# Masks and sink columns of a sliding-window attention section moved from VectorE to half-row TensorE products

## The chip, the cores and the metric

One Trainium2 chip, of which the kernel uses one core. The metric is the device time of one execution in microseconds; lower is better. A core has TensorE (PE, with the loading of its stationary operand shown apart as PEld), VectorE (DVE), ScalarE (ACT), GpSimd (POOL) and SyncE (SP), which run in parallel and meet at semaphores.

## What is computed

Two transformer blocks, one after the other, on 512 tokens of width 1024 in float32. The first has a gated linear attention, a pooling branch and a mixture of 16 experts. The second block has two layers, and each layer runs three attention branches, a cross attention to a memory of 256 tokens, and a gated feed-forward part. The change touches only the first branch of each of these two layers, a sliding-window attention of 8 heads with a window of 128 and one learned sink per head:

```python
mask = (kpos <= t) & (kpos > t - window) & (kpos >= 0)
s = jnp.einsum('bqgrd,bkgd->bgrqk', qb, kb).astype(jnp.float32) * (d ** -0.5)
p = masked_probs(s, mask, sink)      # the sink joins the maximum and the denominator
o = jnp.einsum('bgrqk,bkgd->bqgrd', p.astype(vb.dtype), vb)
```

With blocks of 128 queries, a block sees its own 128 keys under a causal mask and the 128 keys before it under the opposite mask ("recent": only those keys count whose place in their block is after the query's place in its own). The first block has no block before it.

## The kernel before

The kernel is one program with an instruction stream written out by hand for each engine. Attention is cut into units. `units()` (L525) lists them for one layer: section 0 is the sliding-window branch and has 16 units, in the order query block 3, 2, 1, 0 and within a block the head pairs t = 0 to 3. A unit computes two heads, `side` 0 and 1, whose scores lie in two PSUM banks. Twelve units have 256 keys (`nk` 256), the last four have 128. Section 1 (28 units of the sparse branch), section 2 (latent attention) and section 3 (cross attention) follow later in the layer.

Each of PE, DVE and ACT has its own `attend(sec)` that walks over the units in steps s. A step of PE (L1324) issues, in this order:

- the score products of unit s: for each side one product of 64 rows (side 0 on rows 0 to 63, side 1 on rows 64 to 127) and nk columns, then `scored`;
- the transposes of unit s-2, two for each block of keys and side (L1352), after a wait for `scaled` of that unit;
- the products of the probabilities with the values for unit s-3, after a wait for `turned_out`;
- in steps 0, 1, 3, 4, 8 and 9 of section 0, half of a tile of the value projection (`v_behind`, four products of 408 columns, operands `ring,h`).

After step 16 of section 0 come four products of the next stage (`merge_head`), then the last two units, then `merge`. A float32 product appears in the trace as two loads and two matmuls, a transpose as one of each.

A step of DVE (L2533) for unit s in section 0 adds the mask to both sides in PSUM (L2559), copies the two sink values into column nk of the two banks (L2573), drains, and takes the negated row maximum over nk + 1 columns (L2578, `biased`). Then for unit s-1 it waits for `exped`, takes the reciprocal of the sum (L2599) and scales the probabilities (L2605, `scaled`). In steps 1, 5 and 10 it also copies a finished value tile. ACT takes the exponential of unit s (L1763) and copies the transposed probabilities of unit s-1 out of PSUM (L1773).

Section 1 already leaves its causal mask to PE: `barred` is true there, and four more products on 64 rows each add it to the scores in PSUM. Two of them have 128 columns and two have 64; the stationary operand is the upper or lower half of the identity (`ident`) or of the identity turned by 64 (`crossed`), and the moving operand is a half of the rows of the mask itself (`cst`). The products of side 0 use rows 0 to 63 and those of side 1 rows 64 to 127.

Of the kernel before, what the change touches and what calls it, by code (L numbers as in the profile page):

```python
# [17 lines left out]
ALU = mybir.AluOpType  # L18
# [3 lines left out]
P = 128  # L22
# [14 lines left out]
MASKED = -1e30  # L37
# [122 lines left out]
def columns(parts):  # L160
    at, n = {}, 0
    for name, width in parts:
        at[name] = (n, width)
        n += width
    return at, n


CST, N_CST = columns([("ident", P), ("ones", P), ("recent", P), ("causal", P), ("barred", 64), ("crossed", P),
                      ("cmp_add", TT * CB), ("freq", 1), ("freqM", 1),
                      ("sign", 1), ("signM", 1), ("eps", 1), ("eps2", 1)])  # L170
CS1, N_CS1 = columns([("maskf", P), ("maskb", P), ("scan", 768)])
# [8 lines left out]
def constants():  # L180
    c = np.zeros((P, N_CST), np.float32)
    r = np.arange(P)

    def put(arr, at, name, v):
        o, w = at[name]
        arr[:, o:o + w] = v

    put(c, CST, "ident", np.eye(P))
    put(c, CST, "ones", 1.0)
    put(c, CST, "barred", MASKED)  # L190
    put(c, CST, "crossed", np.roll(np.eye(P), 64, axis=0))
    put(c, CST, "causal", np.where(r[None, :] <= r[:, None], 0.0, MASKED))
    put(c, CST, "recent", np.where(r[None, :] > r[:, None], 0.0, MASKED))
    t = np.arange(T).reshape(TT, P)
    ok = (16 * np.arange(NCMP)[None, None, :] + 31) <= t[:, :, None]
    add = np.full((TT, P, CB), MASKED / 10, np.float32)
    add[:, :, 0:NCMP] = np.where(ok, 0.0, MASKED)
    put(c, CST, "cmp_add", add.transpose(1, 0, 2).reshape(P, -1))
    f = (np.float32(10000.0) ** (-np.arange(32, dtype=np.float32) / np.float32(32))).astype(np.float32)
    put(c, CST, "freq", f[r % 32][:, None])  # L200
    f = (np.float32(10000.0) ** (-np.arange(16, dtype=np.float32) / np.float32(16))).astype(np.float32)
    put(c, CST, "freqM", f[r % 16][:, None])
    put(c, CST, "sign", np.where(r % 64 < 32, -1.0, 1.0)[:, None])
    put(c, CST, "signM", np.where(r % 32 < 16, -1.0, 1.0)[:, None])
    put(c, CST, "eps", EPS)
    put(c, CST, "eps2", EPS * EPS)
    c1 = np.zeros((P, N_CS1), np.float32)
    same = (r[:, None] // CHUNK) == (r[None, :] // CHUNK)
    put(c1, CS1, "maskf", same & (r[:, None] <= r[None, :]))
    put(c1, CS1, "maskb", same & (r[:, None] >= r[None, :]))  # L210
    put(c1, CS1, "scan", (np.arange(768) % CHUNK != 0)[None, :])
    ce = np.zeros((P, N_CSE), np.float32)
    put(ce, CSE, "iota", np.arange(CAP)[None, :])
    put(ce, CSE, "cidx", (r % CAP)[:, None])
    sel = np.zeros((P, 8, P), np.float32)
    for p in range(8):
        sel[2 * p, p, :64] = 1.0
        sel[2 * p + 1, p, 64:] = 1.0
    put(ce, CSE, "pairsel", sel.reshape(P, -1))
    inv = np.zeros((4, ROWS, COLS), np.float32)  # L220
    for i, w in enumerate(WINDOWS):
        n = [np.clip(np.arange(m) + w // 2, 0, m) - np.clip(np.arange(m) - w // 2, 0, m) for m in (ROWS, COLS)]
        inv[i] = 1.0 / (n[0][:, None] * n[1][None, :])
    return c, c1, ce, np.ascontiguousarray(np.broadcast_to(inv.reshape(1, -1), (P, 4 * T)))


def two_blocks(nc, stream, xT_d, ctxT_d, memT_d, pos_d, cst_d, cs1_d, cse_d, inv_d, pr1_d, pr2_d, out_d):
    ctx = ExitStack()
    with ctx:
# [10 lines left out]
        cst = sb("cst", [P, N_CST])  # L240
# [169 lines left out]
        def c_(name):  # L410
            o, w = CST[name]
            return cst[:, o:o + w]
# [112 lines left out]
        def units():  # L525
# [5 lines left out]
            def pair(sec, qt, nk, kind, qk, values, outs, first=True, final=True, sink=None, gate=None, end=False, joins=False):  # L531
                nb = nk // P
                u, j = (out[-1], 1) if joins else (None, 0)
                pv = [(outs[i][0], outs[i][1], values[i][b], i, slice(nk * j + P * b, nk * j + P * b + P),
                       first and b == 0, final and b == nb - 1)
                      for b, i in ([(b, i) for b in range(nb) for i in range(2)] if sec < 3 else
                                   [(b, i) for i in range(2) for b in range(nb)])]
                barred = sec == 1
                s = [[(i, slice(nk * j, nk * j + nk), q, k, part is qk[0] and j == 0, part is qk[-1] and not barred)
                      for i, (q, k) in enumerate(part)] for part in qk]  # L540
                if barred:
                    low, high, o, to = slice(0, 64), slice(64, P), CST["causal"][0], nk * (j + 1)
                    s.append([(0, slice(to - P, to), c_("ident")[low, :], cst[low, o:o + P], False, False),
                              (1, slice(to - P, to), c_("crossed")[high, :], cst[high, o + 64:o + 64 + P], False, False),
                              (0, slice(to - 64, to), c_("crossed")[low, :], cst[low, o:o + 64], False, True),
                              (1, slice(to - 64, to), c_("ident")[high, :], cst[high, o + 64:o + P], False, True)])
                if joins:
                    u["subs"], u["nb"], u["end"] = 2, 2 * nb, end
                    u["s"] = [a + b for a, b in zip(u["s"], s)]
                    u["gate"] = u["gate"] and u["gate"] + [gate]  # L550
                    u["pv"] += pv
                    return
                out.append(dict(sec=sec, qt=qt, nk=nk, nb=nb, subs=1, kind=kind, sink=sink, gate=gate and [gate], end=end,
                                s=s, pv=pv))
# [1373 lines left out]
        def _(dve):  # L1928
# [575 lines left out]
            for l in range(LAYERS):  # L2504
# [22 lines left out]
                def attend(sec, between=None):  # L2527
# [7 lines left out]
                    for s in range(len(us) + 1):  # L2535
                        if s < len(us):
# [17 lines left out]
                                                  ALU.add).then_inc(biased, 1)  # L2554
                            else:
                                w = nk
                                if u["kind"] == "window":
                                    o = CST["causal"][0] + P - nk
                                    dve.tensor_tensor(S[:, :, 0:nk], S[:, :, 0:nk],  # L2559
                                                      cst[:, o:o + nk].rearrange("p (g c) -> p g c", g=1)  # L2560
                                                      .to_broadcast([P, 2, nk]), ALU.add)
                                elif u["kind"] == "causal" and u["sec"] == 2:
                                    if u["subs"] == 1:
                                        dve.tensor_tensor(S[:, :, nk - P:nk], S[:, :, nk - P:nk],
                                                          c_("causal").rearrange("p (g c) -> p g c", g=1)
# [4 lines left out]
                                                          .to_broadcast([P, 2, 2, P]), ALU.add)  # L2570
                                if u["sink"] is not None:
                                    w = nk + 1
                                    dve.tensor_copy(S[:, :, nk:w], p2("sinks").rearrange("p (g t) -> p g t", g=2)  # L2573
                                                    [:, :, u["sink"]:u["sink"] + 1])
                                if u["sec"] in (0, 2):
                                    dr()  # L2576
                                if u["subs"] == 1:
                                    ins = dve.tensor_reduce(nbias[:, n % 4, 0:2], S[:, :, 0:w], AX.X, ALU.max, negate=True)  # L2578
# [580 lines left out]
```

## Time and profile before

| | us |
|---|---|
| median of 3 runs | 3275.41 |
| the three runs | 3275.16, 3275.41, 3279.26 |
| the profiled execution, its own time | 3284.84 |
| span of its trace, first to last instruction | 3283.0 |
| PE busy in that span | 3187.8 (97%) |
| DVE busy | 1488.1 (45%) |
| section 0 of the first layer in the trace | from 1078.6 to about 1134.8 |
| section 0 of the second layer in the trace | from 2195.6 to about 2254.0 |

Times in the rows below are microseconds from the span's start in the one profiled execution. The profiled execution took 9.43 us longer than the median of the runs. In a row of the timeline the second number is how long the merged group lasted, from the start of its first to the end of its last instruction, so neighbouring groups overlap; the distance between two starts is what the argument uses. The granted clock of 1.00 is 2.4 GHz, 0.50 is 1.2 GHz.

### The profile page before, as it was taken

The page shows a single profiled execution, that of the slowest core. Times are in us where ns is not written, and L with a number is a line of the kernel's source. Part 1 is how long each engine was busy: PE and PEld are TensorE (multiplying, and loading weights), DVE is VectorE, ACT ScalarE, POOL GpSimd, SP SyncE. Part 2 cuts the span into 40 slices and gives each one's busy share as a digit, 9 for nine tenths or more (in the row PEclk, how much of TensorE's full clock was granted, in tenths as well). Part 3 has the DMA queues.
Part 4 walks back from the last instruction along what each step waited for, and adds up shares of the span by engine and source line. Part 5 has one row for each costly group of instructions (what it writes and reads, how often), then busy time and mean ns, then how long its engine had stood idle before and what let it go on. Part 6 is the DMA issues. An engine that isn't in the chain of part 4 may idle for free.

```text
span 3283.0 us, 39520 instructions
## 1 busy us (share of the span) xinstructions
PE 3187.8 (97%) x15880; PEld 2133.4 (65%) x15880; DVE 1488.1 (45%) x2914; ACT 677.7 (21%) x1393; POOL 142.6 (4%) x100
## 2 busy tenths in 40 slices
PE   7999999999999899999999999999999999999998
PEld 2445784444433575855865888857578478578887
DVE  2244663221113645736634454446375376255533
ACT  2032221000003415423021000023271231210000
POOL 3400010000000000000000000000000000000000
PEclk9999999999999899999999999999999999999999
DMA  7241247999995121121221222311201112222221
GB/s 298 100 160 40 77 170 302 409 406 387 404 409 225 45 84 52 40 77 33 77 90 68 87 89 87 106 62 65 96 9 69 66 52 83 72 77 87 94 84 71
DMA packets 120149, 435.86 MB, mean 133 GB/s; under 512 B 13216, under 2 KB 15008, under 8 KB 119200
## 3 DMA queue, kind: packets, MB, share of 16 engines
q1 hardware_dynamic: 114768, 417.91, 34.1%
q10 hardware_dynamic: 5200, 15.43, 1.2%
q8 instruction: 127, 2.08, 0.3%
q14 instruction: 54, 0.44, 0.0%
HBM read 429.09 MB, written 4.19 MB: 132 GB/s over the span
## 4 chain that ended last, share of the span: by engine, by line
PE 92%; DVE 4%; ACT 2%; issue 1%; DVEq 1%; DMA 1%; ACTq 0%; SPq 0%
PE bank L688 90%; PE bank L1352 1%; DMA ring<-in_stream 1%; DVE arena L2578 1%; DVE arena L2605 0%; DVE arena L2580 0%; DVE bank L2559 0%; DVE arena L2142 0%; PE bank L1347 0%; ACT arena L1722 0%; DVEq L2576 0%; ACT arena L1798 0%; DVE arena L2179 0%; PE bank L1195 0%; DVE arena L2608 0%
## 5 line engine op out<-in xcount | busy, mean ns | idle before, releaser
L688 PE MATMUL bank<-arena 128*128 128x256 f32 (+12 forms) x5520 | 931.3, 375 | 32.7 <-issue 9.7
L688 PEld LDWEIGHTS bank<-arena 128*128 128x128 f32 (+4 forms) x5520 | 624.2, 172 | 290.3 <-issue 166.8
L688 PE MATMUL bank<-h,ring 128*128 128x256 f32 (+1 forms) x1936 | 630.8, 477 | 1.6 <-issue 1.3
L688 PEld LDWEIGHTS bank<-h,ring 128*128 128x128 f32 x1936 | 365.6, 191 | 224.5 <-issue 192.7
L688 PE MATMUL bank<-arena,ring 128*128 128x256 f32 (+2 forms) x1872 | 498.3, 419 | 3.3 <-DVE y L2064 1.8
L688 PEld LDWEIGHTS bank<-arena,ring 128*128 128x128 f32 (+1 forms) x1872 | 332.9, 186 | 151.0 <-issue 107.4
L688 PE MATMUL bank<-ring,arena 128*64 128x512 f32 (+2 forms) x976 | 227.4, 603 | 18.0 <-ACT arena L1568 11.7
L688 PE MATMUL bank<-y,arena 128*128 128x256 f32 (+1 forms) x1064 | 239.0, 381 | 0.0
L688 PE MATMUL bank<-y,ring 128*128 128x256 f32 (+1 forms) x800 | 227.1, 439 | 0.0
L688 PEld LDWEIGHTS bank<-y,arena 128*128 128x128 f32 x1064 | 202.1, 190 | 29.2 <-issue 1.9
L1923 POOL TENSOR_TENSOR sq<-sq 128x512 f32<-128x512 f32 (+1 forms) x56 | 75.1, 1342 | 3072.1 <-ACT sq L1549 3072.1
L688 PEld LDWEIGHTS bank<-y,ring 128*128 128x128 f32 x800 | 151.9, 190 | 69.0 <-issue 53.8
L688 PEld LDWEIGHTS bank<-ring,arena 128*64 128x64 f32 (+2 forms) x976 | 70.8, 137 | 159.5 <-issue 138.0
L1763 ACT ACTIVATE arena<-bank,arena 128x256 f32<-128x256 f32 (+5 forms) x288 | 141.9, 506 | 127.1 <-DVE arena L2578 77.0
L1549 ACT ACTIVATE sq<-x 128x512 f32<-128x512 f32 x64 | 40.1, 630 | 423.1 <-DVEq L2882 256.8
L1773 ACT ACTIVATE arena<-bank 128x1024 f32<-128x1024 f32 (+3 forms) x120 | 92.7, 772 | 118.0 <-PE bank L1352 112.9
L2481 DVE TENSOR_TENSOR arena<-arena,bank 128x512 f32<-128x512 f32 x16 | 11.0, 689 | 194.2 <-PE bank L688 194.2
L688 PE MATMUL bank<-h,arena 128*128 128x256 f32 (+2 forms) x408 | 94.5, 475 | 0.8 <-ACT arena L1722 0.8
L1935 DVE COPY arena<-bank 128x512 f32<-128x512 f32 (+4 forms) x51 | 33.4, 654 | 135.3 <-PE bank L688 132.9
L2892 DVE TENSOR_TENSOR x<-x,bank 128x256 f32<-128x256 f32 x48 | 20.2, 421 | 160.0 <-PE bank L688 159.4
L2578 DVE TENSOR_REDUCE arena<-bank 128x2 f32<-128x514 f32 (+3 forms) x80 | 72.4, 905 | 33.3 <-PE bank L688 29.7
L1352 PE MATMUL bank<-cst,arena 64*128 64x64 f32 x1216 | 61.5, 233 | 19.5 <-DVE arena L2605 16.2
(327 smaller groups left out, 2770.6 us busy)
## 6 DMA issues: line engine op xcount, KB each, us to landing
ring<-in_stream SPq DMA_DIRECT2D x581, 512.0 KB, 4.5
arena<-in_stream SPq DMA_DIRECT2D x132, 512.0 KB, 13.1
h<-in_stream SPq DMA_DIRECT2D x42, 512.0 KB, 11.9
sig<-in_stream SPq DMA_DIRECT2D x21, 512.0 KB, 11.9
sq<-in_stream SPq DMA_DIRECT2D x21, 512.0 KB, 12.3
x<-in_xT ACTq DMA_DIRECT2D x1, 2048.0 KB, 11.2
arena<-memory_kv ACTq DMA_DIRECT2D x4, 512.0 KB, 6.8
outT<-h ACTq DMA_DIRECT2D x8, 256.0 KB, 2.1
```

Of the source, the lines that this page charges most:

```text
L688: ins = pe.matmul(out, lhsT, rhs, start=start, stop=stop, skip_group_check=loose)
L1352: ins = pe.transpose(bank[:, 4 + i, at:at + 64], probs[r, n % 3, side, P * b:P * b + P], c_("ident")[r, r])
L1549: act.activation(sq[:, min(k, 1), 0:width], src(k), ACT.Square).then_inc(squared, 1)
L1763: ins = act.activation(probs[:, n % 3, side, c], bank[:, 2 * (n % 2) + side, c], ACT.Exp, bias=nbias[:, n % 4, i:i + 1], accum_out=den[:, ...
L1773: act.activation(probsT[:, n % 2, :, 0:P * u["nb"]], bank[:, 4:6, 0:P * u["nb"]], ACT.Copy).then_inc(turned_out, 1)
L1923: pool.tensor_tensor(sq[:, 0, 0:width], sq[:, 0, 0:width], sq[:, 1, 0:width], ALU.add).then_inc(added, 1)
L1935: dve.tensor_copy(out, N.bank(n)[0:m, 0:width] if src is None else src).then_inc(N.taken_sem, 1)
L2481: dve.tensor_tensor(acts[:, 512 * half:512 * half + 512], sg[:, half, :], bank[:, 2 + half, :], ALU.mult).then_inc(a_ready, 1)
L2578: ins = dve.tensor_reduce(nbias[:, n % 4, 0:2], S[:, :, 0:w], AX.X, ALU.max, negate=True)
L2892: dve.tensor_tensor(xq[:, part, :], xq[:, part, :], bank[:, b, 0:H2], ALU.add).then_inc(down_taken, 1)
```

## The change

The constants get one more field, `barred_low`: 64 columns of the mask value, ahead of `recent`, so that the shifted slices of `recent` can be read as the ones of `causal` are. `barred` becomes true for section 0 too. For a unit with 256 keys four products add the recent mask on the first 128 key columns (128, 64, 64 and 128 columns); for every unit with a sink four products of one column write the two sinks into column nk; then the four causal products follow, as in section 1. DVE no longer adds the window mask, no longer copies the sinks, and no longer drains in section 0. Its reduction over nk + 1 columns and everything else stay.

```diff
-CST, N_CST = columns([("ident", P), ("ones", P), ("recent", P), ("causal", P), ...
+CST, N_CST = columns([("ident", P), ("ones", P), ("barred_low", 64), ("recent", P), ("causal", P), ...
+    put(c, CST, "barred_low", MASKED)
...
-                barred = sec == 1
+                barred = sec < 2
...
                 if barred:
                     low, high, o, to = slice(0, 64), slice(64, P), CST["causal"][0], nk * (j + 1)
+                    same, other = [c_("ident")[r, :] for r in (low, high)], [c_("crossed")[r, :] for r in (low, high)]
+                    if kind == "window" and nk == 2 * P:
+                        s.append([(0, slice(0, P), other[0], cst[low, o - P - 64:o - 64], False, False),
+                                  (1, slice(0, 64), other[1], cst[high, o - 64:o], False, False),
+                                  (0, slice(0, 64), same[0], cst[low, o - P:o - 64], False, False),
+                                  (1, slice(0, P), same[1], cst[high, o - P:o], False, False)])
+                    if sink is not None:
+                        s.append([(i, slice(nk, nk + 1), block_, p2("sinks")[r, 4 * i + sink:4 * i + sink + 1], False, False)
+                                  for blocks_ in ((same[0], other[1]), (other[0], same[1]))
+                                  for i, (r, block_) in enumerate(zip((low, high), blocks_))])
...
-                                if u["kind"] == "window":
-                                    o = CST["causal"][0] + P - nk
-                                    dve.tensor_tensor(S[:, :, 0:nk], S[:, :, 0:nk],
-                                                      cst[:, o:o + nk].rearrange("p (g c) -> p g c", g=1)
-                                                      .to_broadcast([P, 2, nk]), ALU.add)
-                                elif u["kind"] == "causal" and u["sec"] == 2:
+                                if u["kind"] == "causal" and u["sec"] == 2:
...
                                 if u["sink"] is not None:
                                     w = nk + 1
-                                    dve.tensor_copy(S[:, :, nk:w], p2("sinks").rearrange("p (g t) -> p g t", g=2)
-                                                    [:, :, u["sink"]:u["sink"] + 1])
-                                if u["sec"] in (0, 2):
+                                if u["sec"] == 2:
                                     dr()
```

## Rows read from the trace of the kernel before

**Rows 1.** The page: what the chain that ended last is made of.

```profile
PE 92%; DVE 4%; ACT 2%; issue 1%; DVEq 1%; DMA 1%; ACTq 0%; SPq 0%
```

**Rows 2.** Timeline, a step with value products beside it and the next without (PE loads).

```profile
1097.23 0.30 PEld L688 LDWEIGHTS bank<-arena 64*128 64x128 f32 x4 [0.58 <-issue]
...
1098.10 0.42 PEld L688 LDWEIGHTS bank<-arena 128*64 128x64 f32 x8 
...
1098.69 0.30 PEld L688 LDWEIGHTS bank<-arena 64*128 64x128 f32 x4 [0.17 <-issue]
```

**Rows 3.** Timeline of a later step of section 0, first layer.

```profile
1100.64 0.69 DVE L2559 TENSOR_TENSOR bank<-bank,cst 128x512 f32<-128x512 f32 x1 
...
1101.46 0.69 DVE L2578 TENSOR_REDUCE arena<-bank 128x2 f32<-128x514 f32 x1 
...
1102.27 0.62 DVE L2605 TENSOR_SCALAR arena<-arena 128x256 f32<-128x256 f32 x2 
...
1102.80 0.69 DVE L2559 TENSOR_TENSOR bank<-bank,cst 128x512 f32<-128x512 f32 x1 
...
1102.94 0.33 PEld L1352 LDWEIGHTS bank<-cst,arena 64*128 64x128 f32 x8 [1.37 <-DVE arena L2605]
```

**Rows 4.** Waits in section 0, first layer: us in total, times, longest.

```profile
PEld bank L1352 <- DVE arena L2605: 9.5, 8, 2.0
```

**Rows 5.** The same of section 0 of the second layer.

```profile
PEld bank L1352 <- DVE arena L2605: 9.0, 8, 2.0
```

**Rows 6.** DVE's groups by form in 1078 to 1133: busy us, mean ns; idle before.

```profile
L2559 DVE TENSOR_TENSOR bank<-bank,cst 128x512 f32<-128x512 f32 x12 | 8.3, 693 | 9.4 <-PE bank L688 9.4
...
L2573 DVE COPY bank<-arena 128x2 f32<-128x2 f32 x16 | 2.4, 152 | 0.0
...
L2559 DVE TENSOR_TENSOR bank<-bank,cst 128x256 f32<-128x256 f32 x4 | 1.7, 430 | 2.0 <-PE bank L688 2.0
```

**Rows 7.** Timeline of PE loads in section 1, a joined unit with eight mask products.

```profile
1345.46 0.98 PEld L688 LDWEIGHTS bank<-cst 64*128 64x128 f32 x16 
1346.30 0.38 PEld L1352 LDWEIGHTS bank<-cst,arena 64*128 64x128 f32 x8 
```

**Rows 8.** Timeline of PE loads: eight score products of 32 columns on 64 rows.

```profile
1293.35 0.97 PEld L688 LDWEIGHTS bank<-arena 64*128 64x128 f32 x16 [0.17 <-issue]
1294.34 0.57 PEld L1352 LDWEIGHTS bank<-cst,arena 64*128 64x128 f32 x16 
1294.97 0.14 PEld L688 LDWEIGHTS bank<-arena 128*64 128x64 f32 x2 
```

**Rows 9.** Timeline: four products of 16 columns on 128 rows, in the first block.

```profile
485.24 1.04 PE L688 MATMUL bank<-arena,tmp 128*128 128x16 f32 x8 [0.91 <-DVE tmp L2383]
```

**Rows 10.** Windows: length, busy us (instructions) of PE, PEld, DVE, ACT, POOL, granted clock, DMA share, GB/s.

```profile
1117.00:1119.70 2.70, 1.66 (x20) 1.23 (x20) 2.52 (x9) 2.09 (x6) 0.00 (x0) 0.79 0.95 357
1119.70:1132.20 12.50, 11.65 (x76) 8.26 (x72) 6.04 (x25) 5.93 (x22) 0.00 (x0) 0.50 0.16 65
...
1134.80:1141.00 6.20, 6.17 (x21) 5.16 (x22) 5.33 (x10) 1.19 (x3) 0.00 (x0) 0.72 0.01 3
...
2206.00:2212.00 6.00, 6.00 (x32) 3.21 (x30) 1.76 (x6) 1.66 (x6) 0.00 (x0) 0.72 0.00 0
...
2221.00:2229.00 8.00, 7.52 (x43) 4.91 (x44) 4.62 (x14) 4.38 (x15) 0.00 (x0) 0.57 0.00 0
...
2241.00:2246.00 5.00, 4.70 (x46) 3.44 (x46) 3.69 (x16) 3.16 (x14) 0.00 (x0) 0.66 0.23 89
2246.00:2254.00 8.00, 5.69 (x34) 3.51 (x33) 3.94 (x14) 3.64 (x10) 0.00 (x0) 0.79 0.00 0
```

**Rows 11.** Windows in section 1, among its joined units.

```profile
1340.00:1345.00 5.00, 5.00 (x90) 4.54 (x88) 3.14 (x11) 3.92 (x18) 0.00 (x0) 1.00 0.00 0
```

**Rows 12.** DMA issues: KB and us to landing.

```profile
cst<-in_cst ACTq DMA_DIRECT2D x1, 419.0 KB, 13.1
```

**Rows 13.** The chain that ended last, its first piece: start us, us, what.

```profile
1.64 12.81 DMA ring<-in_stream
```

More of the change, by code:

```diff
@@ L165, in columns @@
     return at, n
-CST, N_CST = columns([("ident", P), ("ones", P), ("recent", P), ("causal", P), ("barred", 64), ("crossed", P),
+CST, N_CST = columns([("ident", P), ("ones", P), ("barred_low", 64), ("recent", P), ("causal", P), ("barred", 64), ("crossed", P),
                       ("cmp_add", TT * CB), ("freq", 1), ("freqM", 1),
```

## The prediction, on record before the changed kernel was run

> **What bounds the kernel now.** I read the page first. The chain that ended last is TensorE for 92 parts in 100 [rows 1], so nearly every microsecond that PE gains or loses is a microsecond of the kernel. VectorE is busy for less than half of the span, and taking work from it helps only where PE waits for it. Section 0 is such a place. So the next view was the timeline of its steps.
>
> Six of the sixteen steps carry half a value tile and leave DVE time. A step without one shows PE alone: the scores of one unit start at 1097.23, the value products of another at 1098.10, the next scores at 1098.69 [rows 2]. That is 1.46 us of PE for a unit of 256 keys. DVE needs more. Its mask addition starts at 1100.64 and the next one at 1102.80 [rows 3], so 2.16 us go by for a unit, and in the meantime PE's transposes stand for 1.37 us until the probabilities are scaled. The waits view adds this up: PE's loads for the transposes stood 9.5 us for L2605 in the first layer and 9.0 us in the second [rows 4, 5]. I take the loads' rows and not those of the matmuls, because the end of a matmul row runs past the time at which the next load could have begun.
>
> The last view is the granted clock. It drops to the lower of its two levels, 1.2 GHz, in and after stretches where PE stood waiting: 12.5 us at 0.50 in the first layer, and parts of four windows in the second [rows 10]. Before the first of these drops lies a window in which PE was busy for 1.66 of 2.70 us [rows 10].
>
> **What DVE loses.** For a unit the reduction starts 0.82 us after the addition (1100.64 to 1101.46 [rows 3]). That is what addition, copy of the sinks and drain cost in a row; alone they are 693 and 152 ns [rows 6]. DVE's step goes from 2.16 to 1.34 us. For the four small units the addition takes 430 ns [rows 6] and the same argument holds.
>
> **What PE gains in work.** No row shows the recent mask or the sinks on PE, but rows show the same kind of product: 64 rows, stationary of 128 columns, two sides on two halves of the rows. Eight mask products of 128 and 64 columns, of section 1, take from 1345.46 to 1346.30 [rows 7], which is 0.42 us for four. I take 0.42 for the four causal products and 0.42 for the four recent ones, which have the same columns in another order. The sinks are four products of one column. The nearest row in rows and sides is that of eight products of 32 columns, 1293.35 to 1294.34, or 0.50 us for four [rows 8]; that distance includes a short gap at its end. From below, sixteen single loads with their transposes took 1294.34 to 1294.97 [rows 8]; eight of them, as many as four float32 products have, are 0.31 us. From above, four products of 16 columns on all 128 rows took 1.04 us [rows 9]. I take 0.44 us, nearer to the row that has the same halves. The same low bound of 0.31 holds for each mask group.
>
> The Trainium skill has a rule that speaks against this part. Its page "TensorE: Matmul & The Clock Gate", section "LDWEIGHTS (loading the stationary operand)", says that a load takes the number of stationary columns over 1.2 GHz, however few rows it has; for 128 columns that is 107 ns, so a product of one column is not cheap. For four products, eight loads, an estimate from it is 0.85 us one after the other and 0.43 us where the two halves of the rows load at once. The trace agrees with the second [rows 8]. By the first the total below would be 13 us higher (32 groups of sinks, 0.41 us each), by the second the same.
>
> So a unit of 256 keys costs PE 0.42 + 0.44 + 0.42 = 1.28 us more, a unit of 128 keys 0.44 + 0.42 = 0.86. A layer has twelve and four: 15.4 + 3.4 = 18.8 us. Two layers: **37.6 us** more for PE.
>
> **What PE gets back, first part: the waits.** PE's step becomes 1.46 + 1.28 = 2.74 us, DVE's 1.34. PE is then the bound in every step, and the waits of 9.5 and 9.0 us have no cause left. One remains in each layer: in step 16 there are no more scores, and PE needs the scaling of unit 14, which stands on DVE behind the reduction of unit 15. From the end of the last scores these are about 0.4 + 0.7 us, against 0.6 us of transposes and value products; with the semaphores I leave 0.6 us. Credit: 18.5 - 1.2 = **17.3 us**.
>
> **Second part: the clock.** What the lower clock costs is PE's busy time in each window times the missing share of the clock [rows 10]: 0.3 + 5.8 + 1.7 in the first layer and 1.7 + 3.2 + 1.6 + 1.2 in the second, 15.6 us. With PE at work throughout it should stay at 2.4 GHz. Joined units of section 1, with PE full of just such products, ran at 1.00 [rows 11]. But the drops belong to one execution, which took 9.4 us longer than the median of the runs, and an execution may have fewer of them; nor do loads of a column's product fill the array. I take three quarters of it, **11.7 us**.
>
> **The sum.** 37.6 - 17.3 - 11.7 = +8.6 us. Against the profiled execution's own 3284.84 us (span 3283.0) this gives 3293.4; the median of the runs lies 9.43 us lower, so 3275.41 + 8.6 = **3284.0 us**, or 0.26% slower.
>
> **Edits costed at nothing.** Constants: 64 more columns are 32 KB beside 419 KB that land in 13.1 us [rows 12], 1 us at the very most if bytes alone set that time and nothing else were loading; they come beside the weights of the ring, on which the chain stands for its first 12.81 us [rows 13]; with that cover gone it would be that 1 us. The reduction still spans nk + 1 columns. Ring slots: the score products no longer end a group, so one that frees ring slots may do so a product earlier; SP's loads start no later than now, relative to PE. If PE's section grows, they have more time. After section 0 nothing is late that PE does not issue itself: the merge's weights, read from SP's queue, come earlier against PE.
>
> **The rivals.**
>
> *The clock does not come back.* Half the added time is products that move one column or 64, and the drops may have another cause than the waits. Then the sum is 37.6 - 17.3 = +20.3 us: 3295.7. For it: drops are found where PE was still 60 to 85% busy. Against it: rows 11.
>
> *The one-column product is dear.* If the sinks cost what the 16-column row does, 1.04 instead of 0.44 us, 32 groups add 19 us: +27.8 us, 3303. Against it: that row uses all 128 rows, where no two loads can run beside each other. A half of it is likelier than all, +18.
>
> *Half-row products hide in each other: faster.* This is one mechanism: loads of one half of the rows run wholly under the other half's stream. At the price of the transposes' loads, 0.31 us for each of 88 groups of four (44 a layer), the work is 27.3 us and the sum is 27.3 - 17.3 - 11.7 = -1.7 us. It gets faster than the bound of 0.2% (-6.6 us) only from 22.4 us of added work down, 0.25 us for each group of four. The sinks at nothing and the masks at 0.32, the stream of their columns, would do: 17.9 us, so -11.1 us, 3264. For it: the halves do overlap already. Against it: eight mask products next to each other take 0.84, which is 0.42 for four, not 0.25.
>
> *Hidden after all: no change.* With the whole clock back (15.6) and the 88 groups at 0.39 each, the sum is 34.3 - 17.3 - 15.6 = +1.4 us: 3276.8. PE's added work then is just paid by its waits and its clock.
>
> **Chances and range.** A change of 0.2% is 6.6 us, about what a measurement of this kernel can tell from no change. PE-bound with most of the clock back, sum between -2 and +14 us: 0.67, of which 0.36 lies above +6.6 and 0.31 below; the clock not back, 0.13, slower; sinks dear, 0.07, slower; hidden after all, 0.06, same; faster than the bound, 0.07. Together slower 0.56, same 0.37, faster 0.07. The range takes in the lower bound of the product costs (-1.7) and goes up to the lost clock (+20.3): 3274 to 3296. Both signs lie in it; the likeliest case alone is 3274 to 3289.
>
> **What would show it.** Right, in the trace after: the transposes' waits for L2605 fall from 9.5 and 9.0 us to about 1 us a layer; a step between two value tiles lasts 2.7 us from scores to scores; section 0 lasts 60 to 62 us instead of 56 and 58; DVE now waits for PE's scores in every step; the granted clock stays at 1.00 from 1080 to the end of the section. Wrong: a window at 0.50 in section 0 (the clock's credit), eight loads of the sinks over much more or less than 0.44 us (the size of the product), or PE's loads still waiting for DVE (the mechanism).

## The result and the profile after

| | before | changed |
|---|---|---|
| median, same chip, us | 3279.26 (5 runs, 3275.16 to 3283.99) | 3293.10 (5 runs, 3291.67 to 3294.07) |
| ratio of the times | | 1.0042, 95% interval 1.0027 to 1.0057 |
| the profiled execution, its own time | 3284.84 | 3293.10 |
| its mean granted clock | 0.990 | 0.996 |
| section 0, first layer | 56.2 | 62.04 (1078.71 to 1140.75) |
| section 0, second layer | 58.4 | 62.03 (2199.82 to 2261.85) |

The change makes the kernel slower, by 13.8 us in the medians of this comparison and by 8.3 us between the two profiled executions. That these two numbers differ is the main thing to explain. One run of the twelve of e3 below took 3748.28 us at a granted clock of 0.846, a slower state of the chip, and stands in its range and median but in no ratio, mean or clock.

In the kernel after, L688 has become L699, L1352 L1363, L2578 L2582 and L2605 L2609. The page's chain gives one part in a hundred more to PE and one less to DVE than [rows 1]:

```profile
PE 93%; DVE 3%; ACT 2%; issue 1%; DVEq 1%; DMA 1%; ACTq 0%; SPq 0%
```

The timeline of PE's loads, one step between two value tiles, for [rows 2] and [rows 3]:

```profile
1104.59 0.30 PEld L699 LDWEIGHTS bank<-arena 64*128 64x128 f32 x4 [0.17 <-issue]
1104.91 0.63 PEld L699 LDWEIGHTS bank<-cst 64*128 64x128 f32 x8 
1105.46 0.53 PEld L699 LDWEIGHTS bank<-arena,cst 64*128 64x128 f32 x8 
1105.90 0.53 PEld L699 LDWEIGHTS bank<-cst 64*128 64x128 f32 x8 
1106.30 0.39 PEld L1363 LDWEIGHTS bank<-cst,arena 64*128 64x128 f32 x8 
...
1107.34 0.30 PEld L699 LDWEIGHTS bank<-arena 64*128 64x128 f32 x4 [0.17 <-issue]
```

Read the distances between starts. The scores start at 1104.59 and those of the next unit at 1107.34: a step is 2.75 us. The sinks' eight loads take from 1105.46 to 1105.90, 0.44 us. The causal ones take 0.40 to the transposes, and the recent ones, which stand behind the scores of 256 columns, 0.55. The transposes, which stood there before, give back 0.10: their eight loads take 0.45 to the next start (1106.30 to 1106.75) where they took 0.55 before (1097.55 to 1098.10). No bracket stands at the transposes: they wait for nothing.

PE's waits in section 0 of the first layer, us in total, times and longest, for [rows 4]:

```profile
PEld bank L1363 <- DVE arena L2609: 0.9, 1, 0.9
```

The second layer has the same 0.9 where [rows 5] had 9.0. DVE's own waits in the same stretch:

```profile
DVE arena L2582 <- PE bank L699: 29.3, 15, 4.3
```

DVE now waits for PE's scores, 29.3 us in the first layer and 31.1 in the second.

The windows over section 0 of both layers, for [rows 10] (the column before the DMA share is the granted clock):

```profile
1078.00:1145.00 67.00, 64.90 (x719) 49.61 (x718) 32.74 (x82) 28.47 (x90) 3.88 (x3) 1.00 0.09 33
2195.00:2265.00 70.00, 67.91 (x726) 50.98 (x725) 32.15 (x82) 28.39 (x91) 0.00 (x0) 1.00 0.11 39
```

PE holds 2.4 GHz throughout. In the same two windows the profiled execution before had 0.87 and 0.88.

The DMA of the constants carries 451.0 KB now and lands 13.9 us after its issue, 0.8 later than in [rows 12], and the chain's first piece now ends at 15.30 instead of 14.45 [rows 13]. Section 0 nevertheless starts at 1078.71 instead of 1078.59, and in e11, which is the same kernel, at 1078.03, so almost nothing of this reaches it.

### The profile page after: what moved, and what is told of

It reads as the page before. It is cut to its first block, busy times and chain, and to the rows that moved or that the text cites. A ratio compares the mean times of both kernels' runs of the same rounds, so it can differ in the third digit from the quotient of the medians.

```text
span 3291.3 us, 40833 instructions
## 1 busy us (share of the span) xinstructions
PE 3205.4 (97%) x16584; PEld 2162.0 (66%) x16584; DVE 1467.6 (45%) x2850; ACT 674.7 (20%) x1393; POOL 142.3 (4%) x100
## 4 chain that ended last, share of the span: by engine, by line
PE 93%; DVE 3%; ACT 2%; issue 1%; DVEq 1%; DMA 1%; ACTq 0%; SPq 0%
PE bank L699 91%; PE bank L1363 1%; DMA ring<-in_stream 1%; DVE arena L2584 0%; DVE arena L2609 0%; PE bank L1358 0%; ACT arena L1733 0%; DVE arena L2582 0%; DVE arena L2190 0%; DVE arena L2612 0%; DVE arena L2416 0%; DVEq L2419 0%; ACT arena L1784 0%; ACT arena L1774 0%; ACT arena L1809 0%
## 5 line engine op out<-in xcount | busy, mean ns | idle before, releaser
L699 PE MATMUL bank<-arena 128*128 128x256 f32 (+12 forms) x5520 | 925.0, 373 | 33.0 <-issue 9.7
L699 PEld LDWEIGHTS bank<-arena 128*128 128x128 f32 (+4 forms) x5520 | 620.1, 170 | 288.9 <-issue 167.1
L699 PE MATMUL bank<-h,ring 128*128 128x256 f32 (+1 forms) x1936 | 627.6, 475 | 1.6 <-issue 1.3
L699 PEld LDWEIGHTS bank<-h,ring 128*128 128x128 f32 x1936 | 363.8, 190 | 223.6 <-issue 192.6
L699 PE MATMUL bank<-arena,ring 128*128 128x256 f32 (+2 forms) x1872 | 498.3, 419 | 3.3 <-DVE y L2075 1.8
L699 PEld LDWEIGHTS bank<-arena,ring 128*128 128x128 f32 (+1 forms) x1872 | 332.9, 186 | 151.1 <-issue 107.5
L699 PE MATMUL bank<-ring,arena 128*64 128x512 f32 (+2 forms) x976 | 227.3, 603 | 19.7 <-ACT arena L1579 12.5
L699 PE MATMUL bank<-y,arena 128*128 128x256 f32 (+1 forms) x1064 | 239.0, 381 | 0.0
L699 PE MATMUL bank<-y,ring 128*128 128x256 f32 (+1 forms) x800 | 227.1, 439 | 0.0
L699 PEld LDWEIGHTS bank<-y,arena 128*128 128x128 f32 x1064 | 202.1, 190 | 29.2 <-issue 1.9
L699 PEld LDWEIGHTS bank<-y,ring 128*128 128x128 f32 x800 | 151.9, 190 | 69.0 <-issue 53.8
L699 PEld LDWEIGHTS bank<-ring,arena 128*64 128x64 f32 (+2 forms) x976 | 71.0, 137 | 161.0 <-issue 139.8
L2582 DVE TENSOR_REDUCE arena<-bank 128x2 f32<-128x514 f32 (+3 forms) x80 | 72.4, 905 | 91.3 <-PE bank L699 90.2
L699 PE MATMUL bank<-h,arena 128*128 128x256 f32 (+2 forms) x408 | 94.5, 475 | 0.8 <-ACT arena L1733 0.8
L699 PEld LDWEIGHTS bank<-cst 64*128 64x128 f32 x960 | 68.3, 190 | 14.3 <-issue 8.6
## 6 DMA issues: line engine op xcount, KB each, us to landing
arena<-in_stream SPq DMA_DIRECT2D x132, 512.0 KB, 12.5
sq<-in_stream SPq DMA_DIRECT2D x21, 512.0 KB, 11.7
```

The lines of the kernel that those rows point to most:

```text
L699: ins = pe.matmul(out, lhsT, rhs, start=start, stop=stop, skip_group_check=loose)
```

## The experiments

e1 is the kernel before and e11 the changed one, both without an edit. All others were made from the changed kernel by a function `on_tensor(i, nk)`, which names the parts that PE adds for unit i of section 0: the recent mask, the sinks, the causal mask. DVE adds or copies the rest as before, each mask only over its own columns, and drains if anything of a unit is left to it (e8 apart, which has no drain in section 0). "Clock" is the mean over the runs of the granted clock of a whole execution; "section 0" is that of the first layer in the profiled execution; "waits" are those of PE's transposes for DVE's scaling in the two layers.

| run | median us (lowest to highest, runs) | ratio [95%] | clock | section 0 | waits |
|---|---|---|---|---|---|
| the change | 3293.10 (3291.67 to 3294.07, 5) | 1.0042 [1.0027, 1.0057] | 0.9958 | 62.04 | 0.9 / 0.9 |
| e1 before again | 3275.12 (3273.52 to 3285.43, 12) | 0.9994 [0.9982, 1.0005] | 0.9935 | 53.07 | 10.1 / 9.8 |
| e2 causal, short steps | 3274.01 (3270.78 to 3276.15, 12) | 0.9986 [0.9976, 0.9996] | 0.9950 | 51.54 | 5.1 / 5.4 |
| e3 sinks on DVE | 3283.94 (3281.21 to 3748.28, 12) | 1.0016 [1.0007, 1.0026] | 0.9947 | 55.84 | 1.6 / 1.6 |
| e4 wide sinks | 3294.77 (3293.55 to 3296.36, 6) | 1.0052 [1.0037, 1.0068] | 0.9952 | 62.04 | 0.9 / 0.9 |
| e5 filler | 3279.55 (3277.87 to 3283.07, 12) | 1.0005 [0.9995, 1.0015] | 0.9947 | 53.97 | 7.2 / 7.2 |
| e6 leveled | 3274.51 (3271.39 to 3277.38, 12) | 0.9989 [0.9979, 0.9999] | 0.9950 | 51.00 | 4.6 / 4.7 |
| e7 sinks only | 3284.95 (3279.79 to 3289.76, 12) | 1.0022 [1.0012, 1.0033] | 0.9928 | 56.04 | 5.0 / 5.0 |
| e8 nothing added | 3262.49 (3261.82 to 3264.85, 6) | 0.9954 [0.9941, 0.9967] | 0.9947 | 45.98 | 4.2 / 4.2 |
| e9 sinks only, wide | 3281.81 (3279.14 to 3287.60, 12) | 1.0010 [1.0000, 1.0019] | 0.9944 | 54.79 | 5.2 / 5.3 |
| e10 causal in all | 3277.78 (3276.51 to 3281.99, 11) | 0.9994 [0.9985, 1.0002] | 0.9947 | 53.10 | 3.8 / 4.1 |
| e11 the change again | 3294.64 (3292.36 to 3295.78, 5) | 1.0045 [1.0032, 1.0059] | 0.9952 | 62.04 | 0.9 / 0.9 |
| e12 e2 again | 3273.60 (3271.00 to 3275.16, 12) | 0.9985 [0.9976, 0.9994] | 0.9952 | 51.53 | 5.1 / 5.4 |

**e1: the kernel before, run again.** No edit. The question was whether executions of one and the same kernel differ by their clock.

> The kernel before, unchanged, to read the granted clock of each of its runs. Theory A (the clock's credit was mis-sized because the one profiled execution had more time at the lower clock than most timed runs): the runs differ from each other, and a run's time follows its clock, about 3.3 us for each 0.001 of the mean clock; the faster runs show 0.993 or more, where the trace of before showed 0.990. Rival (the profiled execution is simply longer by its recording, and all runs have the same 15.6 us of lost clock): all runs show 0.990 and the spread has nothing to do with the clock. Ratio to the kernel before: 1.000.

They do. The runs of before from all comparisons, these twelve among them, are 99, and in groups by the mean clock of the execution:

| clock | runs | mean us |
|---|---|---|
| 0.990 | 17 | 3284.5 |
| 0.991 | 20 | 3283.8 |
| 0.992 | 6 | 3279.3 |
| 0.993 | 8 | 3279.0 |
| 0.994 | 21 | 3275.8 |
| 0.995 | 27 | 3274.0 |

A straight line through the 99 gives 2.25 us for each 0.001, less than the 3.3 expected. The mean over all is 3278.9. The execution profiled before the prediction, with 0.990, is of the slowest kind. This run's profiled execution took 3275.30 at 0.995. Its windows at the places of the first two of [rows 10]:

```profile
1117.00:1119.70 2.70, 1.67 (x22) 1.19 (x22) 2.52 (x9) 2.09 (x7) 0.00 (x0) 0.91 0.91 337
1119.70:1132.20 12.50, 9.71 (x87) 6.90 (x86) 8.62 (x31) 7.96 (x26) 0.00 (x0) 0.88 0.15 61
```

Where the clock was 0.50 for 12.5 us it is now 0.88, and PE shows 9.71 us of work in place of 11.65, with more instructions done. The waits are no shorter, 10.1 instead of 9.5. So the waits were there in both executions and the drop mostly in one.

Where the 9.5 us between the two spans lie is read from PE's timeline, from the first scores of a section 0 to the first loads of `merge` behind it. The first layer's section lasted 56.21 us at 0.990 and 53.07 now, the second's 58.41 and 52.92 (2191.53 to 2244.45). That is 8.6 of the 9.5; another 0.7 lies between the two sections. The row of the loads of the first `merge` in this run's timeline:

```profile
1131.50 3.33 PEld L688 LDWEIGHTS bank<-arena 128*128 128x128 f32 x16 [1.57 <-issue]
```

In the execution before the prediction the same sixteen loads, at 1134.80, took 5.01 us. The two lengths are a second sign of the clock at the end of the section. So the runs differ by their clock, and the rival that all had lost the same is gone.

**e2: the causal mask alone, and only in steps without a value tile.** It takes from PE the sinks and the recent mask, and relieves DVE where PE had waited.

```diff
-    return ("recent", "sink", "causal")
+    return () if i in (0, 1, 3, 4, 8, 9) else ("causal",)
```

> Only the causal mask goes to TensorE, and only in the ten units whose step has no value tile beside it; recent mask and sinks stay on VectorE there, and the other six units are as before. Theory (two loops of 1.46 and 2.16 us that should be made level): PE's step goes to 1.88 us and DVE's to about 1.9, so section 0 is 1 to 2.5 us shorter a layer at full clock, and with fewer waits there are fewer drops of the clock: 2 to 10 us less than before in all, ratio 0.997 to 0.9995. Rival (any work added to PE lengthens the kernel by itself, 10 x 0.42 us a layer): 4 to 8 us more, ratio 1.001 to 1.0025.

```profile
PEld bank L1371 <- DVE arena L2628: 5.1, 7, 1.8
```

This waits row (L1371 are the transposes here, L2628 the scaling) has half of before's. The clock is 1.00 in windows over section 0 of both layers, and no run is below 0.994. The mean is 3274.1, level with the runs of before that have 0.995; so the gain over before as a whole goes with the lower clocks, which no longer occur.

**e3: the sinks given back to DVE.**

```diff
-    return ("recent", "sink", "causal")
+    return ("recent", "causal")
```

> The change, with the four sink products taken back out of it; VectorE copies the sinks and drains as before. Theory (a one-column product costs PE its weight loads, 0.44 us for the four): PE's step is 2.31 instead of 2.75 us, 16 x 0.44 = 7 us a layer less than in the whole change, so 14 us less in all and about level with the kernel before (ratio 0.999 to 1.001). Rival (one column costs next to nothing, the masks are what costs): within 2 us of the whole change, ratio 1.0035 to 1.005.

Its timeline of PE's loads, a step as above:

```profile
1102.66 0.30 PEld L707 LDWEIGHTS bank<-arena 64*128 64x128 f32 x4 [0.17 <-issue]
1102.98 1.08 PEld L707 LDWEIGHTS bank<-cst 64*128 64x128 f32 x16 
1103.92 0.39 PEld L1371 LDWEIGHTS bank<-cst,arena 64*128 64x128 f32 x8 
...
1104.97 0.30 PEld L707 LDWEIGHTS bank<-arena 64*128 64x128 f32 x4 [0.17 <-issue]
```

The step is 2.31 us, 0.44 less, and the sections of the two layers are 6.2 and 5.8 us shorter, 12.0 together; of the 14.1 for 32 groups of sinks the longer waits (1.6 against 0.9 a layer) take 1.4 back. The mean over the runs is 3283.8, only 9.7 below the change's ten runs, and I had expected 14. The ratio of 1.0016 lies above the 0.999 to 1.001 of the theory, and further below the 1.0035 of the rival. The clock is a little lower than with the change, 0.9947 against 0.9955, at 2.25 us for 0.001 another 1.8 us. Together that accounts for all but about 1 us of the miss.

**e4: sink products of 64 columns instead of one.** The bank's columns behind nk are not read, so the extra ones change nothing else.

```diff
-(i, slice(nk, nk + 1), block_, p2("sinks")[r, 4 * i + sink:4 * i + sink + 1], False, False)
+(i, slice(nk, nk + 64), block_, pr2[r, PR2["sinks"][0] + 4 * i + sink:PR2["sinks"][0] + 4 * i + sink + 64], False, False)
```

> The change, with each sink product 64 columns wide instead of one (the 63 more columns of PSUM are read by nobody). Theory (the weight loads set the pace): the group of four still takes 0.42 to 0.45 us, time within 1.5 us of the whole change (ratio to before about 1.004). Rival (the moving columns count too): 0.107 us a product on each half of the rows, 0.21 us a group, 32 groups, 7 us more than the whole change (ratio 1.006).

PE's loads in its timeline, and its group of sink matmuls by form in section 0 (busy us, mean ns):

```profile
1106.22 0.30 PEld L707 LDWEIGHTS bank<-arena 64*128 64x128 f32 x4 [0.17 <-issue]
...
1107.09 0.53 PEld L707 LDWEIGHTS bank<-arena,cst 64*128 64x128 f32 x8 
1107.54 0.53 PEld L707 LDWEIGHTS bank<-cst 64*128 64x128 f32 x8 
...
1108.97 0.30 PEld L707 LDWEIGHTS bank<-arena 64*128 64x128 f32 x4 [0.17 <-issue]
```

```profile
L707 PE MATMUL bank<-arena,cst 64*128 64x64 f32 x128 | 9.6, 264 | 0.0
```

The changed kernel's own group has one column:

```profile
L699 PE MATMUL bank<-arena,cst 64*128 64x1 f32 x128 | 8.8, 232 | 0.0
```

The step is 2.75 us again and the sinks' group 0.45. Sixty-four times the columns cost nothing in the step. The sections are the same too, 62.04 and 62.03 us. The mean of the six runs, 3294.9, is 1.4 above that of the change's ten and not the rival's 7, and the ratio of 1.0052, above the expected 1.004, has no cause in section 0: in the profiled execution the section only starts 1.64 us later, at 1080.35. So the price does not lie in the moving columns. That it lies in the eight loads, and not in something else that each product brings with it, no run separates.

**e5: before, with four unread mask products in each of the ten short steps.** It takes nothing from DVE; only the constants are those of the changed kernel. If only PE's idleness made the clock fall, this should hold it.

```diff
+                if sec == 0 and len(out) not in (0, 1, 3, 4, 8, 9):
+                    o = CST["causal"][0]
+                    s.append([(i, slice(3 * P, 4 * P), c_("ident")[r, :], cst[r, o:o + P], False, False)
+                              for _ in range(2) for i, r in enumerate((slice(0, 64), slice(64, P)))])
```

> The kernel before, with VectorE's work untouched, and four products of 128 columns added on TensorE in the ten units of section 0 whose step has no value tile; they write columns 384 to 511 of the scores' banks, which nobody reads. 0.43 us each, in steps where PE waits 0.4 to 2 us for VectorE anyway. Theory (PE's waits are what lets the clock fall, and runs of before differ by how often it falls): the added work lies in the waits, at most 0.5 us a layer comes on top, and the runs no longer spread: mean clock 0.994 to 0.996 in each, times 3273 to 3278 with none above 3280. Rival (the drops have nothing to do with PE's waits): the runs spread over 12 us as those of before do, with clocks from 0.990 to 0.995, and the median is that of before plus 0 to 5 us.

The clock's spread is much smaller: nine runs at 0.995, two at 0.994, one at 0.993. But the time is 3280, where by its clock before would have 3274 to 3275, so the filler costs 5 us or more and not the 1 or less that I expected. The timeline of a step, PE's loads and DVE's addition only (L2585 here), with the first loads of `merge`:

```profile
1098.14 0.30 PEld L711 LDWEIGHTS bank<-arena 64*128 64x128 f32 x4 [0.58 <-issue]
1098.46 0.63 PEld L711 LDWEIGHTS bank<-cst 64*128 64x128 f32 x8
...
1099.34 0.70 DVE L2585 TENSOR_TENSOR bank<-bank,cst 128x512 f32<-128x512 f32 x1 [2.59 <-PE bank L711]
...
1133.15 5.01 PEld L711 LDWEIGHTS bank<-arena 128*128 128x128 f32 x16 [1.56 <-issue]
```

The addition of the same unit in the kernel before, whose scores start at 1097.23 [rows 2]:

```profile
1097.98 0.70 DVE L2559 TENSOR_TENSOR bank<-bank,cst 128x512 f32<-128x512 f32 x1 [2.15 <-PE bank L688]
```

Filler was meant to run in time that PE would wait anyway. Ten groups of 0.43 are 4.3 us a layer; the waits shrank by 2.9 and 2.6 against e1. DVE's addition waits for the last product of the scores, filler included: it starts 1.20 us after the first load, where it started 0.75 after it before. So the whole group of 0.43 us delays DVE and can come back as a wait. And the clock was not whole: it was 0.97 and 0.95 in windows over section 0 of the two layers (1076 to 1141 and 2193 to 2262), the loads of `merge` took 5.01 us, as in the execution before the prediction, and section 0 of the second layer 55.7 us (e1: 52.9).

**e6: parts chosen by the room in each unit.** Units 0, 6, 7, 11, 13 and 15 give PE one to three parts, the others none.

```diff
+    return {0: ("causal",), 6: ("recent", "causal"), 7: ("recent", "causal"), 11: ("recent", "sink", "causal"),
+            13: ("causal",), 15: ("causal",)}.get(i, ())
```

> Parts moved to TensorE unit by unit, so that the two loops come out level: the causal mask in units 0, 13 and 15, both masks in 6 and 7, both masks and the sinks in 11, nothing elsewhere. A recurrence over the steps, with the durations of the rows, gives 2.6 us a layer less than before at full clock, where the causal mask in the ten short steps gave 1.2. Theory (what counts is PE's wait at each step, and it can be filled or emptied unit by unit): 3269 to 3271, ratio 0.997 to 0.998. Rival (the waits move on to the next step and what is moved is lost): not below the 3274 of the causal mask alone.

3274.51, no better than e2. I had expected 3269 to 3271. The first layer's section is 0.5 us shorter than in e2. The second layer's is 0.8 longer, 52.73 against 51.88, at a clock of 0.97 where e2 had 1.00. The choice of units gave no more than this.

**e7: only the sinks on PE.**

```diff
-    return ("recent", "sink", "causal")
+    return ("sink",)
```

> Only the sinks go to TensorE, in all sixteen units; VectorE adds both masks. Theory (a load is paid whatever the columns): 0.44 us more of PE in each of 32 units, of which the twenty short steps have room for it in their waits, VectorE 0.2 us less a unit: at equal clock 2 to 4 us slower than before (about 3277 at a clock of 0.995), and 0.999 to 1.0005 in the ratio, since the clock falls less. Rival (one column costs next to nothing): 2 to 4 us faster than before at equal clock, about 3271.

The waits halve to 5.0, nearly as in e2, but the clock does not come back: the runs go from 0.990 to 0.995, with a mean of 0.9928, and the time from 3279.79 to 3289.76. The two runs at 0.995 took 3281.1, some 7 us above before at that clock, where I expected 2 to 4. So waits of the same size went with two different clocks. The chip is not the reason: e5, e6 and e8 ran on the same one, with waits of 7.2, 4.6 and 4.2 us, and have 0.9947, 0.9950 and 0.9947.

**e8: nothing added.** It leaves out both masks and the sinks of section 0 altogether, on DVE and on PE, and with them DVE's drain, and the reduction covers nk columns instead of nk + 1. It measures what all of this work is worth.

```diff
-    return ("recent", "sink", "causal")
+    return ()
...
-                         [(r, slice(P * t, P * t + P)) for r in half], sink=t, end=t == 3)
+                         [(r, slice(P * t, P * t + P)) for r in half], sink=None, end=t == 3)
...
-                                if u["kind"] == "window":
+                                if u["kind"] == "never":
```

> Masks and sinks of section 0 are left out, on both engines (the result of this branch then lacks them): this shows what all of it costs in the kernel. Theory (PE's waits for VectorE in section 0 come from these additions): the waits of 9.5 and 9.0 us fall to 2 to 3 us a layer, 7 us a layer less at equal clock, 3258 to 3262, ratio 0.994 to 0.9955. Rival (the waits come from the reduction and the scaling, which stay): 3270 to 3274, ratio 0.998.

3262.49, just above the 3258 to 3262 that was expected. The four runs at 0.995 have a mean of 3262.9, 11 us below before at that clock. The waits fell less than expected, to 4.2 us a layer and not to 2 to 3, so part of them does not come from the masks and the sinks. With DVE doing it, the whole masking of both layers costs 11 us in the kernel; with PE doing it the change is 31 us above this run.

**e9: only the sinks on PE, with 64 columns.** e7 with e4's edit.

> The run with the sinks alone on TensorE, with each sink product 64 columns wide (63 more columns that nobody reads). PE waits and works for as long as there; only the columns that stream through the array are more. Theory S (what keeps the clock up is streamed columns, not the absence of waits: the sinks alone left 5.0 us of waits a layer and still showed 0.990 to 0.995, where the causal mask in the short steps left 5.1 and showed 0.994 to 0.996): mean clock 0.9945 or more, no run under 0.993, 3281 to 3283 us. Rival W (the waits alone do it, and the spread with the sinks alone was chance): clocks and times as there, mean 0.9928 and 3285 us, runs down to 0.990.

The same loads and waits of nearly the same size (5.2 and 5.3), but more columns streamed: the clock is 0.9944 instead of 0.9928, its lowest run 0.993 instead of 0.990, and the mean time 3282.5 instead of 3285.0. The profiled execution had 1.00 and 0.90 in section 0 of the two layers, so even here the clock is not safe. The mean clock falls just short of the 0.9945 of theory S; the lowest run and the median time are as it said. Taken with e7 it speaks for what PE streams, and not its waits alone, as part of what holds the clock. It does not show it: the difference is small, rests on twelve runs each, and the two ran on different chips (the 29 runs of before beside them had mean clocks of 0.9931 beside e7 and 0.9926 beside e9, so the chip does not favour e9). And where PE has the masks too, the width of the sinks makes no difference: 0.9955 with one column, 0.9952 with 64 (e4).

**e10: the causal mask on PE in all units.**

```diff
-    return ("recent", "sink", "causal")
+    return ("causal",)
```

> Only the causal mask goes to TensorE, in all sixteen units; recent mask and sinks stay on VectorE. Theory (PE pays 0.42 us in each unit; in the six steps with a value tile there is no wait to pay it from): the ten short steps as in the run with those alone, and 6 x 0.42 = 2.5 us a layer more, less about 1 us of waits behind them: 2 to 4 us above 3274, so 3276 to 3278, at clocks of 0.994 to 0.996. Rival (VectorE is the bound all the time, so relief in every unit counts): below 3274.

3277.78, 4 us above e2 and e12, as expected. The reason given for it holds only in part. In two of the six steps with a value tile PE did wait in e2, for 1.76 us in step 3 and for 0.61 in step 8; here it waits for 1.10 and not at all. So the six more groups, 2.5 us a layer, are paid in part from waits, which fall by 1.3 in each layer (5.1 to 3.8, 5.4 to 4.1). The sections are 1.6 and 1.5 us longer than in e2. Relief of DVE in these six units buys nothing beyond that.

**e11: the change again, e12: e2 again,** beside the same runs of before.

> The whole change once more, beside more runs of before on another occasion. Theory (at equal clock it costs 18.7 us; runs of before lose 5 us on average to the clock and those of the change do not): 3291 to 3295 in every run, clock 0.995 to 0.996; the ratio to before 1.004 to 1.005, and against only those runs of before that show 0.995 it is 1.0055 to 1.006.

> The causal mask in the ten short steps once more. Theory (section 0 is about 1.5 us a layer shorter at equal clock, and the clock does not fall in it): 3270 to 3277 in every run, ratio 0.998 to 0.9995. Rival (the first result was the chance of a slow set of runs of before): ratio 1.000 or above, or runs above 3280.

Both repeat: the change 3294.64 with a section of 62.04 us, the causal mask in short steps 3273.60. One run of the change, 3295.78, lies above the expected 3295, and one shows a clock of 0.994. The causal mask in short steps is the best version that computes everything, faster than before by 0.15% (0.06 to 0.24%), which is less than the 0.2% that one comparison can tell, though both of its intervals exclude 1.

## Why the prediction came out as it did

The direction, the range and the mechanism held. The likeliest time, 3284.0, was 9 us too low.

**Right: the added work.** A step of 2.74 us was predicted and 2.75 is there. Group by group it is less exact: 0.55, 0.44 and 0.40 us for 0.42, 0.44 and 0.42, less 0.10 at the transposes. The sinks' price of 0.44 us was chosen between rows at 0.31, 0.50 and 1.04 and is met to the hundredth, which is partly luck; e4 shows that it has nothing to do with their width. The Trainium skill, page "TensorE: Matmul & The Clock Gate", section "LDWEIGHTS (loading the stationary operand)", says that a load's time goes by its stationary columns and not by its rows. The trace agrees with this: in section 0 of the changed kernel's first layer loads with 128 columns have a mean of 188 ns on 64 rows and of 189 ns on 128. It does not agree with the page's figure as the price of every load: one lasts 188 ns and not 107, and the eight loads of the transposes took 0.31 us [rows 8] where the estimate from the page is 0.43 with both halves of the rows at once. For the sinks that same estimate, 0.43 us, is the one that the 0.44 and 0.45 us support. With these two measurements the rivals of a dear one-column product and of products hidden in each other are gone: the one needed up to 1.04 us, the other 0.25.

**Right: the waits.** They fell from 9.5 and 9.0 to 0.9 each; that is 1.8 for both layers together where 1.2 was allowed.

**Right: their sum.** 37.6 - 17.3 = 20.3 us. At a clock of 0.995 before takes 3274.0, and the change 3293.5 as the mean of its ten runs (clock 0.9955): 19.5. Its three runs that show 0.995 themselves have 3294.8: 20.9. The sections agree: 62.04 and 62.03 against e1's 53.07 and 52.92 are 18.1 us more, and e1's sections had 0.97 for their 44.4 and 44.4 us of PE work, some 3 us; at one clock that is 21.

**Right in the profile, wrong in the median: the clock.** In section 0 it is 1.00 as predicted, so the rival "the clock does not come back" did not occur as it was worded. The step of the prediction that failed is the size of the credit, "I take three quarters of it, 11.7 us", set against the median of the runs. The 15.6 us were read from one execution, and e1 shows that it was of the kind that lost most: 3284.5 on average at 0.990, 10.5 above 3274.0. Against that execution the sum is right: 3293.4 was worked out and 3293.1 came. How close it came is partly luck, since nothing measured chose the three quarters. Then 9.43 us were taken off for the median of the three runs, but those runs, by their times of 3275.16 to 3279.26 (their clocks are not on record), had already not lost most of that clock. The same microseconds were credited twice. Over all 99 runs before has a mean of 3278.9, so the clock gives back 4.9 us on average, and by the measured difference, 3293.5 - 3278.9 = 14.6 us, it is 20.3 - 14.6 = 5.7. With this in place of 11.7 the sum is +14.6. One reading of the prediction was off as well: "60 to 85% busy" fits two of the seven windows of [rows 10]; in the other five, all with a clock of 0.72 or less, PE was busy for 93% or more of the time.

**The rest of the miss is the base.** The three runs had a median of 3275.41; the mean over all is 3278.9. Of the 9.1 us between 3284.0 and 3293.1, 6.0 are the credit (11.7 less 5.7) and 3.5 the base, less 0.4 by which 3293.1 lies under the mean of the change's ten runs.

**What stays open.** What decides whether an execution of before ends at 0.990 or 0.995. Its waits are alike in both. Open too is whether products of one column hold the clock less well than wider ones. e7 and e9 speak for it, the change and e4 show no such difference, and nothing shows a cause.

## What to carry to other kernels

Before a better clock is credited, compare the mean clock of several executions of the kernel before: if the profiled one is slower than the median, the credit belongs to that execution alone, and a sum made against its own time must not be moved to the median unchanged. A wait on the bounding engine justifies moving only as much work to it as the wait is long: here 18.5 us of waits were paid with 37.6 us of products, while four causal products in the ten short steps of a layer came out level or a little faster. Where the added work stands ahead of what the other engine waits for, even less of it fits: in e5 4.3 us a layer took only 2.9 and 2.6 from the waits. A float32 product of one column cost as much here as one of 64, with a stationary operand of 128 columns, so a small vector copy was the cheaper place for it: back on DVE (e3) it made the kernel 9.7 us faster than the change.

## What the runs showed of the hardware

The kernel before spread over 3272.55 to 3285.76 us, and the execution's mean granted clock orders it: 3284.5 at 0.990, 3274.0 at 0.995. In the change and in e2, e4 to e6 and e8 to e12 no run was under 0.993; e7 has runs down to 0.990.

Four half-row float32 products with stationary operands of 128 columns take 0.44 us with one column and 0.45 with 64. Where only such products were added, the mean clock was 0.9928 with one column (e7) and 0.9944 with 64 (e9), at waits of 5.0 and 5.2 us and on two chips; with the masks added too it was 0.9955 and 0.9952 (e4).

The size of the waits alone did not set the clock: 5.0 us a layer with 0.9928 (e7), 4.6 with 0.9950 (e6) and 7.2 with 0.9947 (e5), on one chip.
